# Column sums and gate broadcasts of a two-layer transformer block moved onto TensorE transposes and VectorE sums

## The chip, the cores and the metric

One core of one Trainium2 chip (trn2). The engines are TensorE (PE, with its weight loads listed apart as PEld), VectorE (DVE), ScalarE (ACT), GpSimd (POOL) and SyncE (SP), which issues the loads. The metric is the time of one execution on the device in microseconds (us), the median of several runs.

## The reference

Two residual blocks run one after the other over 256 tokens of width 1024, everything in fp32. Each block has several sub-blocks (FFN, short convolution, sparse attention, differential attention, grouped attention), and each of these is modulated by vectors that come from a conditioning vector `c` through a 1024 x 1024 slice of a large matrix:

```python
mod = (jax.nn.silu(c) @ ada_w[layer] + ada_b[layer]).reshape(B, 3, 3, D)
h = modulate_pre(x, g[0, 0], mod[:, 0, 0], mod[:, 0, 1])     # rms_norm(x)*(1+scale)+shift
y = swiglu_ffn(h, ffn_w_in[layer, 0], ffn_w_out[layer, 0])
x = x + weight * gate[:, None, :] * rms_norm(y, g_post)      # gated_post_add
...
mod = (cond_lat @ ada_w[i] + ada_b[i])[:, None, :]           # second block: shift, scale, gate x 2
modc = (cond_ctx @ ada_w[i] + ada_b[i])[None, None, :]       # the same matrix with a second vector
```

So there are 32 such products of a vector of 1024 with a 1024 x 1024 matrix, and eleven sub-blocks that use them as `shift`, `scale` and `gate`.

## The kernel before

Weights are streamed in units of 1 MB (128 x 2048 fp32) through a ring of three buffers `stage`. ScalarE rounds a unit to `w_hi` (fp32r, L821), VectorE forms the remainder `w_lo` (L1245), and TensorE makes each product out of three passes, `h_hi*w_hi`, `h_lo*w_hi` and `h_hi*w_lo`: L1948 to L1950 in the first half of a sub-block (`up`), L1999 in the second (`down`). The order on each engine is written out by hand, with semaphores between the engines (`lo_done`, `mid_done`, `ada_sum`, `ada_col` and others). The sub-blocks are, in order: s0 FFN, s1 convolution, s2 FFN, s3 key/value projection, s4 FFN, s5 sparse attention (nsa), s6 FFN, s7 differential attention (diff), s8 FFN over 512 rows, s9 grouped attention (gqa), s10 FFN. FFN `up` steps 0 to 8 are three steps of a loop body, executed once and then twice more in a loop.

**The modulation vectors.** For 23 of the vectors (those of s0, s1, s2, s4, s6 and s8) the product is accumulated by VectorE: eight operations `acc_ops` (L1290, L1292) over tiles 128 x 1024 of `ada`, each scaled by one element of the condition per partition, into a tile 128 x 1024 (`acc`, held in `gate_b`). The vector is the sum of this tile over its 128 partitions. `acc_sum` on TensorE makes this sum with eight matmuls, each with 128 columns of `acc` as its weights and four columns of ones as what moves through; it stands between two halves of a step of products. `acc_col` on VectorE then adds the bias to the eight columns and puts them into `modv` (L1306). In s8 there are two conditions, so each of its three vectors has two tiles and 16 matmuls. Four of the 23 vectors are `late`: their sum stands between two sub-blocks.

**The gates.** A sub-block's output is multiplied by a row of 1024 gate values that must stand on all partitions, while `modv` holds them as columns. VectorE multiplies the identity by each of the eight columns (`diag`, L1472, eight instructions), and TensorE multiplies a matrix of ones by `diag` in two matmuls of 512 columns (L1968), so that each row of the bank is the gate. ScalarE copies the two banks to `gate_b` (L979). This is done 12 times: once per sub-block but s3, and twice in s7 and s8. In an FFN the gate stands in the last `up` step, between products; in s5 and s9 it stands after the second `down` step.

## Time and profile before

| what | value |
|---|---|
| median of 3 runs | 2211.81 us (2211.53 to 2211.98) |
| profiled execution, from first to last instruction (the only time the profile gives for it) | 2215.9 us |
| busy: PE, DVE, ACT, POOL | 2109.6 us (95%), 1375.2 us (62%), 936.4 us (42%), 97.9 us (4%) |
| chain that ended last, by engine | PE 82%; DVE 8%; ACT 4%; DMA 3%; issue 2% |
| HBM read | 408.47 MB, 185 GB/s over the span |
| DMA share and rate from 0 to 50 us, from 50 to 300 us | 0.97 and 350 GB/s; 0.76 and 261 GB/s |

"Busy" is the time in which an engine executed anything. The chain that ended last goes from the last instruction back to what released each one; its shares say which engine's work set the end. A matmul in fp32 that is not a transpose stands as two records, one for each of its passes. Ends of matmuls are modelled, so the pace of TensorE is read from the distance between starts.

### The profile page before, as it was taken

The page shows a single profiled execution, that of the slowest core. Times are in us where ns is not written, and L with a number is a line of the kernel's source. Part 1 is how long each engine was busy: PE and PEld are TensorE (multiplying, and loading weights), DVE is VectorE, ACT ScalarE, POOL GpSimd, SP SyncE. Part 2 cuts the span into 40 slices and gives each one's busy share as a digit, 9 for nine tenths or more (in the row PEclk, how much of TensorE's full clock was granted, in tenths as well). Part 3 has the DMA queues.
Part 4 walks back from the last instruction along what each step waited for, and adds up shares of the span by engine and source line. Part 5 has one row for each costly group of instructions (what it writes and reads, how often), then busy time and mean ns, then how long its engine had stood idle before and what let it go on. Part 6 is the DMA issues. An engine that isn't in the chain of part 4 may idle for free.

```text
span 2215.9 us, 33686 instructions
## 1 busy us (share of the span) xinstructions
PE 2109.6 (95%) x13577; PEld 1849.4 (83%) x13577; DVE 1375.2 (62%) x2012; ACT 936.4 (42%) x1405; POOL 97.9 (4%) x142
## 2 busy tenths in 40 slices
PE   5999999999899999989999999989999999999999
PEld 3998898998899986459987997678888787977997
DVE  3767798677767674447755755866445334856454
ACT  4334435344533454444355445842122223554343
POOL 2000000000100001200001000010000000000000
PEclk8999999999999998889999999999999999999999
DMA  9887686886678756746854321024434232315553
GB/s 327 278 292 276 221 293 220 286 286 245 209 266 304 284 174 227 236 166 228 286 173 140 115 92 43 1 96 139 163 117 151 76 105 76 115 54 194 181 180 114
DMA packets 246618, 411.38 MB, mean 186 GB/s; under 512 B 10237, under 2 KB 191958, under 8 KB 246486
## 3 DMA queue, kind: packets, MB, share of 16 engines
q1 hardware_dynamic: 245888, 409.31, 54.3%
q8 instruction: 93, 1.52, 0.3%
q14 instruction: 40, 0.32, 0.0%
q10 hardware_dynamic: 597, 0.23, 0.0%
HBM read 408.47 MB, written 1.05 MB: 185 GB/s over the span
## 4 chain that ended last, share of the span: by engine, by line
PE 82%; DVE 8%; ACT 4%; DMA 3%; issue 2%; SPq 1%; POOL 1%; DVEq 0%; ACTq 0%
PE bank L1999 20%; PE bank L1948 14%; PE bank L1950 14%; PE bank L1949 14%; PE bank L2074 3%; PE bank L2076 3%; PE bank L2075 3%; PE bank L1900 2%; DVE w_lo L1245 1%; PE bank L1879 1%; DMA ada<-in_ada_w 1%; DVE gate_b L1292 1%; DMA xs<-in_ada_w 1%; PE bank L2178 1%; ACT w_hi L821 1%
## 5 line engine op out<-in xcount | busy, mean ns | idle before, releaser
L1245 DVE TENSOR_TENSOR w_lo<-stage,w_hi 128x2048 fp32r<-128x2048 f32 x255 | 584.6, 2294 | 444.6 <-ACT w_hi L821 443.8
L821 ACT CAST w_hi<-stage 128x2048 fp32r<-128x2048 f32 x255 | 485.5, 1905 | 654.0 <-PE bank L1950 240.7
L1948 PE MATMUL bank<-h_hi,w_hi 128*128 128x256 f32 (+1 forms) x2360 | 712.5, 302 | 2.6 <-ACT mid L994 2.6
L1950 PE MATMUL bank<-h_hi,w_lo 128*128 128x256 f32 (+1 forms) x2360 | 707.1, 300 | 0.0
L1949 PE MATMUL bank<-h_lo,w_hi 128*128 128x256 f32 (+1 forms) x2360 | 707.1, 300 | 0.0
L1948 PEld LDWEIGHTS bank<-h_hi,w_hi 128*128 128x128 f32 x2360 | 454.1, 192 | 19.1 <-issue 5.5
L1949 PEld LDWEIGHTS bank<-h_lo,w_hi 128*128 128x128 f32 x2360 | 454.0, 192 | 15.6 <-issue 1.9
L1950 PEld LDWEIGHTS bank<-h_hi,w_lo 128*128 128x128 f32 x2360 | 453.6, 192 | 14.0
L1999 PE MATMUL bank<-w_hi,h_hi 128*128 128x512 f32 x776 | 245.7, 394 | 8.3 <-DVE h_lo L1254 7.7
L1999 PE MATMUL bank<-w_hi,h_lo 128*128 128x512 f32 x776 | 244.0, 392 | 0.0
L1999 PE MATMUL bank<-w_lo,h_hi 128*128 128x512 f32 x776 | 244.0, 392 | 0.0
L1292 DVE SCALAR_TENSOR_TENSOR gate_b<-ada,cond,gate_b 128x1024 f32<-128x1024 f32 x182 | 231.7, 1283 | 5.5
L1999 PEld LDWEIGHTS bank<-w_hi,h_hi 128*128 128x128 f32 x776 | 145.3, 189 | 41.4 <-issue 11.3
L1999 PEld LDWEIGHTS bank<-w_lo,h_hi 128*128 128x128 f32 x776 | 146.8, 189 | 30.8
L1999 PEld LDWEIGHTS bank<-w_hi,h_lo 128*128 128x128 f32 x776 | 146.7, 189 | 30.9
L2074 PE MATMUL bank<-w_hi,h_hi 128*128 128x256 f32 (+1 forms) x552 | 159.4, 289 | 7.9 <-issue 4.3
L2075 PE MATMUL bank<-w_lo,h_hi 128*128 128x256 f32 (+1 forms) x552 | 157.7, 286 | 0.0
L2076 PE MATMUL bank<-w_hi,h_lo 128*128 128x256 f32 (+1 forms) x552 | 157.6, 285 | 0.0
L1752 DVE TENSOR_TENSOR mid<-silu_t,bank 128x256 f32 (+3 forms) x132 | 60.9, 463 | 150.5 <-PE bank L1950 150.5
L1191 ACT ACTIVATE silu_t<-bank 128x256 f32<-128x256 f32 (+1 forms) x132 | 54.5, 418 | 217.0 <-PE bank L1950 207.1
L2074 PEld LDWEIGHTS bank<-w_hi,h_hi 128*128 128x128 f32 x552 | 107.6, 195 | 9.3 <-issue 7.0
L2075 PEld LDWEIGHTS bank<-w_lo,h_hi 128*128 128x128 f32 x552 | 107.8, 195 | 0.0
(252 smaller groups left out, 2024.7 us busy)
## 6 DMA issues: line engine op xcount, KB each, us to landing
ada<-in_ada_w SPq DMA_DIRECT2D x114, 1024.0 KB, 5.4
stage<-in_ffn_w_in SPq DMA_DIRECT2D x88, 1024.0 KB, 8.7
stage<-in_ffn_w_out SPq DMA_DIRECT2D x44, 1024.0 KB, 5.1
stage<-in_ffn_w_gu SPq DMA_DIRECT2D x44, 1024.0 KB, 5.2
stage<-in_ffn_w_down SPq DMA_DIRECT2D x22, 1024.0 KB, 5.0
stage<-in_a_w_in SPq DMA_DIRECT2D x12, 1024.0 KB, 7.6
stage<-in_diff_w_in SPq DMA_DIRECT2D x12, 1024.0 KB, 5.5
ada<-in_kv_ada_w SPq DMA_DIRECT2D x8, 1024.0 KB, 5.6
```

The lines of the kernel that those rows point to most:

```text
L821: a.copy(w_hi[:, s, :], stage[:, s, :]).then_inc(hi_done, 1)
L1191: a.activation(silu_t[:, q, 0:T], bank[q][:, 0:T], ACT.Silu).then_inc(silu_done, 1)
L1245: v.tensor_tensor(w_lo[:, s, :], stage[:, s, :], w_hi[:, s, :].bitcast(F32), ALU.subtract).then_inc(lo_done, 1)
L1292: ins = v.scalar_tensor_tensor(out=acc[c], in0=w, scalar=cond[:, b, kk, c:c + 1], in1=acc[c], op0=ALU.mult, op1=ALU.add)
L1752: v.tensor_tensor(mid[:, bass.ds(o, T)], silu_t[:, q, 0:T], bank[2 + q][:, 0:T], ALU.mult).then_inc(mid_done, 1)
L1948: m.matmul(dst[:, 0:T], wh, h_hi[:, h0:h0 + T], start=(k == ks[0]), stop=False)
L1949: m.matmul(dst[:, 0:T], wh, h_lo[:, h0:h0 + T], start=False, stop=False)
L1950: ins = m.matmul(dst[:, 0:T], wl, h_hi[:, h0:h0 + T], start=False, stop=(k == ks[-1]))
L1999: ins = m.matmul(y_bank(T, tt, h)[:, :], a_[:, r:r + P], w_[:, slot, kc * D + h * 512:kc * D + (h + 1) * 512], start=first and n == 0, sto ...
L2074: m.matmul(dst, h_hi[:, r], w_hi[:, slot, c], start=(k == ks[0]), stop=False)
L2075: m.matmul(dst, h_hi[:, r], w_lo[:, slot, c], start=False, stop=False)
L2076: ins = m.matmul(dst, h_lo[:, r], w_hi[:, slot, c], start=False, stop=(k == ks[-1]))
```

## The change

1. `acc_sum` of the 19 vectors that are not late issues, for each tile, eight transposes of 128 x 128 (`acc` as weights, the identity moving) into two whole banks. `acc_col` gets a VectorE sum over the free dimension for each tile (`reduce_sum`, from 128 x 1024 in PSUM to 128 x 8 in `astat`), a wait of VectorE for that sum (`acc_red`), and then adds the bias as before. The banks used start at 4, formerly 5. The four late vectors stay as they were.
2. `gate` on TensorE issues eight transposes whose weights are one column of the gate vector read 128 times (step zero). VectorE's eight multiplications with the identity and the wait for them are gone; TensorE now waits for the gate vector itself (`G`, or `ada_col`).
3. One wait of TensorE for `cmp_kept` (a ScalarE copy out of bank 4) is added in the loop of s4.

```diff
+        def reduced(v):
+            late = [s["v"] + s["late"] for s in subs if s["late"]]
+            return len([x for x in made_by_dve(rv(v) + 1) if x not in late])
+        def is_late(v):
+            return v in [s["v"] + s["late"] for s in subs if s["late"]]
...
             def acc_col(vi, z, i=None):
                 dve.wait_ge(ada_sum, rv(vi) + (1 if i is None else i))
+                if not is_late(vi):
+                    for c in range(streams(vi)):
+                        src = bank_all[:, z + 2 * c:z + 2 * c + 2, :].rearrange("p b (k q) -> p (b k) q", q=P)
+                        ins = v.reduce_sum(flat_astat[:, 8 * c:8 * c + 8], src, AX_X)
+                    ins.then_inc(acc_red, 1)
+                    dve.wait_ge(acc_red, reduced(vi) + (0 if i is None else i - 1))
                 for c in range(streams(vi)):
-                    src = bank[z][:, 32 * c:32 * c + 32].rearrange("p (c j) -> p c j", j=4)[:, :, 0]
+                    src = flat_astat[:, 8 * c:8 * c + 8]
+                    if is_late(vi):
+                        src = bank[z][:, 32 * c:32 * c + 32].rearrange("p (c j) -> p c j", j=4)[:, :, 0]
...
-                    gv = modc[:, 2, 8 * st:8 * st + 8]
-                    dve.wait_ge(dve_s, t.at((tag, "G", st)))
-                for h in range(2):
-                    if st:
-                        dve.wait_ge(pe_s, t.at((tag, "gate", st - 1, h)))
-                    for k in range(4):
-                        ins = v.tensor_scalar(diag[:, h, k * P:(k + 1) * P], ident[:, :], gv[:, 4 * h + k:4 * h + k + 1], None, ALU.mult)
-                    t.done(ins, dve_s, (tag, "diag", st, h))
...
                     for c in range(KC):
-                        o = 32 * st + 4 * c
-                        ins = m.matmul(bank[z][:, o:o + 4], acc[st][:, c * P:(c + 1) * P], ones[:, 0:4], start=True, stop=True)
+                        if is_late(vi):
+                            o = 32 * st + 4 * c
+                            ins = m.matmul(bank[z][:, o:o + 4], acc[st][:, c * P:(c + 1) * P], ones[:, 0:4], start=True, stop=True)
+                        else:
+                            ins = m.transpose(bank[z + 2 * st + c // 4][:, c % 4 * P:(c % 4 + 1) * P], acc[st][:, c * P:(c + 1) * P], ident[:, :])
...
             def gate(s, tag, c):
+                if s["post"]:
+                    gv = modc[:, 2, 8 * c:8 * c + 8]
+                    pe.wait_ge(dve_s, t.at((tag, "G", c)))
+                else:
+                    gv = modv[:, mv(s, 2), 8 * c:8 * c + 8]
+                    pe.wait_ge(ada_col, max(rv(mv(s, 2)), rv(s["v"] + 2) if s["dv"] else 0) + 1)
                 for h in range(2):
                     if c:
                         pe.wait_ge(act_s, t.at((tag, "gateb", c - 1, h)))
-                    pe.wait_ge(dve_s, t.at((tag, "diag", c, h)))
-                    t.done(m.matmul(gate_bank(s, h, c)[:, :], ones[:, :], diag[:, h, :], start=True, stop=True), pe_s, (tag, "gate", c, h))
+                    for k in range(4):
+                        ins = m.transpose(gate_bank(s, h, c)[:, k * P:(k + 1) * P], gv[:, 4 * h + k:4 * h + k + 1].broadcast_to([P, P]), ident[:, :])
+                    t.done(ins, pe_s, (tag, "gate", c, h))
...
-                                    acc_col(s["v"], 5, i)
+                                    acc_col(s["v"], 4, i)
...
-                                also = {(0, 1): (lambda: acc_sum(s["v"], 5, i),)}
+                                also = {(0, 1): (lambda: pe.wait_ge(act_s, t.at("cmp_kept")) if after_kv(s) else None, lambda: acc_sum(s["v"], 4, i))}
```

**TensorE, third vector of s0** (step 9 of `up`). Before, the eight matmuls with four columns of ones; `gate_b` is the accumulated tile:

```order
L1949 MATMUL bank<-h_lo,w_hi 128x256
L1950 MATMUL bank<-h_hi,w_lo 128x256
L1900 MATMUL bank<-ones,gate_b 128x4 x8
L1948 MATMUL bank<-h_hi,w_hi 128x256
L1949 MATMUL bank<-h_lo,w_hi 128x256
L1950 MATMUL bank<-h_hi,w_lo 128x256
```

Now, eight transposes at the same place (the lines have moved by 13):

```order
L1962 MATMUL bank<-h_lo,w_hi 128x256
L1963 MATMUL bank<-h_hi,w_lo 128x256
L1913 MATMUL bank<-ident,gate_b 128x128 x8
L1961 MATMUL bank<-h_hi,w_hi 128x256
L1962 MATMUL bank<-h_lo,w_hi 128x256
L1963 MATMUL bank<-h_hi,w_lo 128x256
```

The number of instructions is the same; the columns that move are 128 in place of four.

**TensorE, gate of s0** (last `up` step). Before, two matmuls of 512 columns; `diag` is what VectorE wrote:

```order
L1949 MATMUL bank<-h_lo,w_hi 128x256
L1950 MATMUL bank<-h_hi,w_lo 128x256
L1968 MATMUL bank<-diag,ones 128x512 x2
L1948 MATMUL bank<-h_hi,w_hi 128x256
L1949 MATMUL bank<-h_lo,w_hi 128x256
```

Now, eight transposes of `modc`, which holds the gate vector:

```order
L1962 MATMUL bank<-h_lo,w_hi 128x256
L1963 MATMUL bank<-h_hi,w_lo 128x256
L1987 MATMUL bank<-ident,modc 128x128 x8
L1961 MATMUL bank<-h_hi,w_hi 128x256
L1962 MATMUL bank<-h_lo,w_hi 128x256
```

They are at the same place between the same products.

**VectorE, end of the convolution s1**. Before: the multiplications with the identity (L1472), the first half of a late vector (L1290, L1292), weight remainders, the column sum (L1306):

```order
L1464 SCALAR_TENSOR_TENSOR modc<-modv,cols 128x8
L1472 TENSOR_SCALAR diag<-ident,modc 128x128 x8
L1290 TENSOR_SCALAR gate_b<-ada,cond 128x1024
L1292 SCALAR_TENSOR_TENSOR gate_b<-ada,cond,gate_b 128x1024 x3
L1245 TENSOR_TENSOR w_lo<-stage,w_hi 128x2048
L1306 TENSOR_TENSOR modv<-bank,cols 128x8
L1245 TENSOR_TENSOR w_lo<-stage,w_hi 128x2048 x2
L1254 TENSOR_TENSOR h_lo<-mid,h_hi 128x512
```

Now:

```order
L1482 SCALAR_TENSOR_TENSOR modc<-modv,cols 128x8
L1300 TENSOR_SCALAR gate_b<-ada,cond 128x1024
L1302 SCALAR_TENSOR_TENSOR gate_b<-ada,cond,gate_b 128x1024 x3
L1255 TENSOR_TENSOR w_lo<-stage,w_hi 128x2048
L1311 TENSOR_REDUCE astat<-bank 128x8
L1324 TENSOR_TENSOR modv<-astat,cols 128x8
L1255 TENSOR_TENSOR w_lo<-stage,w_hi 128x2048 x2
L1264 TENSOR_TENSOR h_lo<-mid,h_hi 128x512
```

Eight instructions have gone ahead of the late vector, and one sum over 128 x 1024 (L1311) has come in behind the first of the three remainders.

## Rows read from the trace of the kernel before

**Rows 1.** Costliest groups by line: busy us, mean ns | idle before.

```profile
L1900 PE MATMUL bank<-ones,gate_b 128*128 128x4 f32 x416 | 48.8, 250 | 0.0
L1472 DVE TENSOR_SCALAR diag<-ident,modc 128x128 f32<-128x128 f32 x48 | 10.0, 282 | 0.2
```

**Rows 2.** PE in order of time, a column sum in s0: start us, us.

```profile
84.79 0.28 PE L1950 MATMUL bank<-h_hi,w_lo 128*128 128x256 f32 x1
84.91 1.84 PE L1900 MATMUL bank<-ones,gate_b 128*128 128x4 f32 x16
...
86.82 0.28 PE L1949 MATMUL bank<-h_lo,w_hi 128*128 128x256 f32 x1
```

**Rows 3.** PE in order of time, the gate of s0.

```profile
173.77 1.88 PE L1968 MATMUL bank<-diag,ones 128*128 128x512 f32 x4
...
175.61 0.28 PE L1949 MATMUL bank<-h_lo,w_hi 128*128 128x256 f32 x1
```

**Rows 4.** Line L1959, transposes of activations: ns min/median/max.

```profile
L1959 PE MATMUL bank<-ident,mid x208: 270/273/476, 14.6 to 2015.8; 128*128 128x128 f32 x104
```

**Rows 5.** PE in order of time, one run of such transposes.

```profile
19.37 1.09 PE L1959 MATMUL bank<-ident,mid 128*128 128x128 f32 x8
```

**Rows 6.** PE in order of time, two column sums in s8.

```profile
1570.13 3.63 PE L1900 MATMUL bank<-ones,gate_b 128*128 128x4 f32 x32
1573.62 0.49 PE L1948 MATMUL bank<-h_hi,w_hi 128*128 128x512 f32 x1
...
1640.65 4.62 PE L1900 MATMUL bank<-ones,gate_b 128*128 128x4 f32 x32
1645.13 0.77 PE L1948 MATMUL bank<-h_hi,w_hi 128*128 128x512 f32 x1
```

**Rows 7.** Windows of s8: busy us (count) by engine, PEclk, DMA share, GB/s.

```profile
1574.90:1578.20 3.30, 3.30 (x9) 2.59 (x8) 0.22 (x1) 0.00 (x0) 0.00 (x0) 0.50 0.00 0
1578.30:1581.60 3.30, 3.30 (x16) 2.73 (x15) 0.48 (x1) 0.00 (x0) 0.00 (x0) 1.00 0.00 0
...
1646.50:1649.80 3.30, 3.30 (x9) 2.56 (x8) 0.00 (x0) 0.00 (x0) 0.00 (x0) 0.50 0.00 0
```

**Rows 8.** Windows of s7, in which PE does nothing but transposes (L2312).

```profile
1431.50:1434.80 3.30, 3.30 (x18) 3.26 (x17) 3.30 (x6) 2.46 (x4) 0.00 (x0) 0.50 0.00 0
1434.90:1440.00 5.10, 4.08 (x25) 3.45 (x24) 1.96 (x3) 5.10 (x9) 0.00 (x0) 1.00 0.00 0
```

**Rows 9.** Line L1667, the sums (maxima) over banks: ns min/median/max.

```profile
L1667 DVE TENSOR_REDUCE astat<-bank x32: 681/952/1225, 1356.9 to 1419.9; 128x2 f32<-128x1024 f32 x16, 128x2 f32<-128x512 f32 x16
```

**Rows 10.** DVE in order of time in s0, a weight remainder.

```profile
109.85 2.29 DVE L1245 TENSOR_TENSOR w_lo<-stage,w_hi 128x2048 fp32r<-128x2048 f32 x1
```

**Rows 11.** PE in order of time, first product of that unit.

```profile
115.49 0.28 PE L1948 MATMUL bank<-h_hi,w_hi 128*128 128x256 f32 x1
```

**Rows 12.** DVE in order of time, end of s1.

```profile
318.55 2.29 DVE L1245 TENSOR_TENSOR w_lo<-stage,w_hi 128x2048 fp32r<-128x2048 f32 x1 [0.44 <-ACT w_hi L821]
...
326.39 0.42 DVE L1819 TENSOR_TENSOR mid<-silu_t,bank 128x256 f32<-128x256 f32 x1
```

**Rows 13.** PE in order of time, first `down` step of s1.

```profile
326.12 0.61 PE L1999 MATMUL bank<-w_hi,h_lo 128*128 128x512 f32 x2
326.87 0.50 PE L1999 MATMUL bank<-w_hi,h_hi 128*128 128x512 f32 x1
```

**Rows 14.** PE in order of time, the gate of s5.

```profile
975.83 1.88 PE L1968 MATMUL bank<-diag,ones 128*128 128x512 f32 x4
979.72 0.47 PE L1999 MATMUL bank<-w_hi,h_hi 128*128 128x512 f32 x1 [2.01 <-DVE h_lo L1254]
```

**Rows 15.** ACT in order of time, the second copy of that gate.

```profile
977.74 0.59 ACT L979 COPY gate_b<-bank 128x512 f32<-128x512 f32 x1 [0.27 <-PE bank L1968]
```

**Rows 16.** PE in order of time, the first instruction behind the first gate of s7.

```profile
1426.23 0.83 PE L2297 MATMUL bank<-mid 128*128 128x128 f32 x6
```

**Rows 17.** ACT in order of time beside it.

```profile
1424.66 0.63 ACT L1108 COPY mid<-bank 128x256 f32<-128x256 f32 x2
```

More of the change, by code:

```diff
@@ L112, in trace @@
         acc_s = sem("acc_s")
+        acc_red = sem("acc_red")
         part_done = [sem(f"part_done{i}") for i in range(3)]
@@ L1777, in _ @@
                         if s["dv"] and j == 9:
-                            acc_col(s["v"] + 2, 5)
+                            acc_col(s["v"] + 2, 4)
                         if s["nvec"] == 5:
@@ L1785, in _ @@
                         if j == 3:
-                            acc_col(s["v"], 5)
+                            acc_col(s["v"], 4)
                         split(u + 3 * j + 3)
@@ L2389, in _ @@
                     also = {}
-                    up_step(9, None, 2, (0, 2), False, {(0, 1): (lambda: acc_sum(s["v"] + 2, 5),)} if s["dv"] else None)
+                    up_step(9, None, 2, (0, 2), False, {(0, 1): (lambda: acc_sum(s["v"] + 2, 4),)} if s["dv"] else None)
                     if T == 256:
@@ L2405, in _ @@
                     up_step(1, None, 3, (0, 2, 6), False)
-                    up_step(2, None, 3, (0, 2, 6), False, {(1, 1): (lambda: acc_sum(v0, 5),)})
+                    up_step(2, None, 3, (0, 2, 6), False, {(1, 1): (lambda: acc_sum(v0, 4),)})
                     up_step(3, None, 3, (0, 2, 6), False, {(2, 0): (early_gate,)})
```

## The prediction

> **What bounds the kernel now.** I read the profile from the whole to the part. The busy shares and the chain that ended last come first: TensorE is busy 95% of the span and holds 82% of the chain, so a microsecond taken from TensorE is worth a microsecond wherever it has no wait close behind it. The groups by line show that the column sums are on that engine: 416 records [rows 1], that is 26 tiles x 8 matmuls x 2 passes. 22 of the 26 tiles change (16 with one stream in s0, s1, s2, s4 and s6, six in s8), and four late ones do not. TensorE in order of time then gives the price of one. Products start 0.12 us apart; the column sum starts at 84.91 and the second product behind it at 86.82 [rows 2]. Without the sum that product would start at 85.03, so the sum costs 1.79 us, although hardly any columns move: 16 passes, about 0.11 us apart. No wait stands around it. In the same way a gate costs 175.61 - 173.77 - 0.12 = 1.72 us [rows 3].
>
> **What a transpose costs.** The activations are transposed in fp32 by the same instruction: 26 tiles x 8 make exactly the 208 records of that line [rows 4], so a transpose has one pass, not two. Eight in a row stand for 1.09 us, the last of them 0.27 us long [rows 4, 5]: seven distances in 0.82 us, 0.117 each, and 8 x 0.117 = 0.94 us until the next instruction can start. That was at full clock with nothing to wait for; a run of 16 costs 1.88 us.
>
> **The terms on TensorE.**
> - 16 column sums of one stream: 1.79 - 0.94 = 0.85 each, 13.6 us.
> - Three vectors of s8, 32 passes each. At full clock one takes 1573.62 - 1570.13 = 3.49 us [rows 6] and would take 1.88: 1.61 each for two (the third vector stands like the first), 3.2 us. The one at 1640.65 takes 1645.13 - 1640.65 = 4.48 us [rows 6] since the clock falls within it: 2.6 us. Together 5.8.
> - The clock. Behind two of these three sums the granted clock is 0.50, that is 1.2 instead of 2.4 GHz: nine matmuls in 3.3 us where 16 run at full clock [rows 7]. That costs 3.3 x 7/16 = 1.4 us after 1574.9, and 4.7 x 7/16 = 2.1 us from 1645.1 to 1649.8. What TensorE did before was a sum of 3.5 us in which four columns moved per pass. In s7 TensorE does nothing but fp32 transposes from 1431.5 to 1434.8, at 0.50, and afterwards the clock is 1.00 [rows 8]. So transposes keep it up, and the 3.5 us come back.
> - Gates between products (s0, s2, s4, s6, s10 and both of s8, seven): 1.72 - 0.94 = 0.78 each, 5.5 us.
> - Gates of s5 and s9. Here TensorE stands still behind the gate: it starts at 975.83, and the next product at 979.72 waited for `h_lo` [rows 14]. The wait hangs on the gate itself. ScalarE copies both banks, the second at 977.74, only when the second matmul is done [rows 15], and then rounds what VectorE and TensorE wait for. With transposes the first bank is full after 3 x 0.117 + 0.27 = 0.62 us, the second after 7 x 0.117 + 0.27 = 1.09; the first copy, 0.59 us long, overlaps the second half, so the second copy starts about 1.1 us behind the gate's start instead of 1.91. That is 0.8 each, 1.6 us, and the stall of 2.01 us itself stays.
> - The first gate of s7. The matmuls behind it start at 1426.23 [rows 16], but their input has been copied at 1424.66 + 0.63 = 1425.3 [rows 17]: 0.9 us. Behind the second gate TensorE waits for VectorE until 1431.03, so this one gives nothing.
> - The gate of s1 gives nothing either. There TensorE stands before 326.87 until VectorE's `mid` of 326.39 is done [rows 12, 13], and VectorE works without a wait from 318.55, where it last waited for ScalarE's `w_hi` [rows 12]. That start moves by the 0.85 of the column sum ahead of it; the gate's 0.78 only makes the wait longer.
>
> Sum: 13.6 + 5.8 + 3.5 + 5.5 + 1.6 + 0.9 = 30.9 us.
>
> **The costs on VectorE.** Added are 22 sums over 128 x 1024 in PSUM. The trace has the same shape as a maximum over two banks, up to 1225 ns [rows 9]: 22 x 1.22 = 27 us. Removed are 96 multiplications: 48 of them take 10.0 us [rows 1], so eight take 1.67 and all of them 20 us. VectorE is busy 62%, so the sum of 7 us is covered as long as the single place is. The tightest place is the loop of the FFNs: column sum, four `acc_ops`, and behind them in VectorE's queue the weight remainders for which TensorE waits (`lo_done`). One of these ends at 109.85 + 2.29 = 112.14, and TensorE takes the unit at 115.49 [rows 10, 11]: 3.35 us in hand, which the new 1.22 us, plus the 0.85 by which TensorE comes earlier, do not use up. Were that cover gone, a column sum would cost what it adds there, 1.22 us. In s1 both meet: the eight multiplications (1.67) leave ahead of the late vector and the new sum (1.22) comes in, so that VectorE reaches its wait for `w_hi` no later. The queue of loads has the same slack: `acc_ops` free the `ada` ring, and SyncE issues weight loads behind those of `ada`; but at 261 GB/s, against 350 in the first 50 us, the DMA engines are not the bound, and a pace higher by 2% doesn't make them so. The wait for `cmp_kept` and the gate's wait for `G` or `ada_col` name work that ends microseconds earlier in TensorE's order; I price them at nothing.
>
> **What the trace does not show** is a weight load of one column read 128 times. Its lower bound is the dense transpose, 0.117 us; the nearest row above it is the pace of transposes at half clock, 3.3 / 18 = 0.18. I take the dense one, because as many elements go into the array and the other operand is the same identity; at 0.18 the cost is 96 x 0.07 = 6 us, which the upper end of the range holds.
>
> **The skill.** Rows 8 show the clock rising over transposes. The Trainium skill, "TensorE: Matmul & The Clock Gate", Part 4: PE-mode transpose, says the contrary: transposes do not count as busy time for the clock gate. It also gives about 275 ns for one, and the trace agrees (273), though their pace is what counts. By that rule the sum would lose the 3.5 us of clock, 27.4 in all; its hard form is the last rival.
>
> **The rivals.**
> - The clock behind the sums of s8 stays as it was: 30.9 - 3.5 = 27.4, that is 2184.4 us. Against it: rows 8. Chance 0.09.
> - VectorE's sum comes onto TensorE's path at each place, because a remainder or `mid` is late: 22 x 1.22 = 26.8 given back, 2207.7 us. For it: the sum stands ahead of everything else in VectorE's queue; against it: 3.35 us in hand. Chance 0.05.
> - The read with step zero is slow: at 0.34 us per gate transpose, three times the dense one, 96 x 0.22 = 21 us are given back, 2202 us. Nothing in the trace is near it. Chance 0.06.
> - Slower than before: the granted clock falls behind every run of transposes in the midst of products. The place is the 19 column sums and 12 gates, the price 1.4 us each as behind 1574.9, so 31 x 1.4 = 43 us against 30.9: 2224 us. It decides from 22 of the 31 places on. Against it: the clock rose over transposes [rows 8], and 1.8 us of passes with four columns, which stand there now, are followed by products that are still 0.28 us long, as at full clock [rows 2]. Chance 0.04. The rule of the Trainium skill's page named above would be its reason.
>
> **How the numbers follow.** The profiled execution has 2215.9 us, 4 us above the median of the runs; the sum is made on it and taken from the median: 2211.8 - 30.9 = 2180.9 us, chance 0.73 for this course, with 0.03 for mixtures. Its own spread comes from the clock, which falls at different instants at the ten boundaries between sub-blocks (1.4 to 2.1 us for one fall more or less) and from the pace of a transpose, which I read from one run (10% of it over 22 x 8 + 96 = 272 transposes is 3 us). With the first rival that makes 2172 to 2190. A measurement of this kernel can tell about 0.2%, 4.4 us: all but the last rival are faster by more.
>
> **What would show it.** Right: the new transposes in s0 start about 0.12 us apart, the product behind them comes 0.94 us after the first; no clock of 0.50 in s8 between 1540 and 1720; the new sum on VectorE at 1.2 us, and no new wait of TensorE for `w_lo` in the FFNs; in s1 a longer wait before the second half of the first `down` step; TensorE's busy time lower by about 28 us. Wrong: transposes with two records each, paces of 0.2 us for the gates, windows at 0.50 behind column sums or gates, or TensorE waiting for L1255 or for `modv`.

## The result, and the profile after

The changed kernel takes 2179.72 us (median of 4 runs, 2176.2 to 2183.14) beside 2211.67 for the kernel before on the same chip: ratio 0.9854, 95% interval [0.9836, 0.9872], so 32 us less (28 to 36). Measured a second time it was 2183.04 us, ratio 0.9869 [0.9849, 0.9889], 29 us less. The forecast was 30.9 less, 2180.9 us.

The profiled execution has a span of 2174.5 us, 41.4 less than the profiled one of before. That is 9 to 12 us more than the medians say, so some of it belongs to this pair of executions and not to the change. TensorE is busy for 2060.2 us (before 2109.6), VectorE for 1381.8 (1375.2).

The costliest groups by line, as in [rows 1]; line, operation, count | busy us, mean ns | idle before:

```profile
L1913 PE MATMUL bank<-ident,gate_b 128*128 128x128 f32 x176 | 22.3, 272 | 0.0
L1911 PE MATMUL bank<-ones,gate_b 128*128 128x4 f32 x64 | 7.4, 248 | 0.0
L1987 PE MATMUL bank<-ident,modv 128*128 128x128 f32 x48 | 6.2, 272 | 0.0
L1987 PE MATMUL bank<-ident,modc 128*128 128x128 f32 x48 | 6.2, 272 | 0.0
L1311 DVE TENSOR_REDUCE astat<-bank 128x8 f32<-128x1024 f32 x22 | 26.5, 1218 | 0.0
```

The 352 passes of 22 tiles are 176, one for each transpose, and the four late tiles are left with 64 (L1911). The 96 gate transposes (L1987) are in two halves, from `modc` and `modv`. VectorE's new sum takes 1218 ns.

TensorE in order of time in s0: the first column sum (answers to [rows 2]), the unit of [rows 11], and the gate (answers to [rows 3]).

```profile
82.47 1.04 PE L1913 MATMUL bank<-ident,gate_b 128*128 128x128 f32 x8
83.27 0.36 PE L1961 MATMUL bank<-h_hi,w_hi 128*128 128x256 f32 x1
83.47 0.28 PE L1962 MATMUL bank<-h_lo,w_hi 128*128 128x256 f32 x1
...
112.14 0.28 PE L1961 MATMUL bank<-h_hi,w_hi 128*128 128x256 f32 x1
...
168.57 1.03 PE L1987 MATMUL bank<-ident,modc 128*128 128x128 f32 x8
...
169.56 0.28 PE L1962 MATMUL bank<-h_lo,w_hi 128*128 128x256 f32 x1
```

Read it by differences. From the start of the sum to the second product behind it were 86.82 - 84.91 = 1.91 us [rows 2]; now 83.47 - 82.47 = 1.00. A column sum saves 0.91. Behind a gate the same distance was 175.61 - 173.77 = 1.84 [rows 3] and is 0.99: 0.85. And the lead of the changed kernel grows by just these steps. Its first sum starts 84.91 - 82.47 = 2.44 us earlier, before anything of the change has acted; the unit of [rows 11], one sum later, 115.49 - 112.14 = 3.35 earlier; the gate, three sums later, 173.77 - 168.57 = 5.20 earlier. Three sums are 2.76, 0.92 each. The other sums of one stream are no different: from the start of the sum to the first product behind it are 1.70 or 1.71 us at all 16 places of the kernel before, and 0.79 at all 16 now (here 82.47 to 83.27), 0.91 less.

TensorE in s8, its three column sums (the first two answer to [rows 6]), and the windows there (answers to [rows 7]; us, then busy (count) of PE, PEld, DVE, ACT, POOL, then the granted clock, DMA share, GB/s).

```profile
1544.02 1.91 PE L1913 MATMUL bank<-ident,gate_b 128*128 128x128 f32 x16
1545.69 0.48 PE L1961 MATMUL bank<-h_hi,w_hi 128*128 128x512 f32 x1
...
1611.07 1.91 PE L1913 MATMUL bank<-ident,gate_b 128*128 128x128 f32 x16
1612.73 0.47 PE L1961 MATMUL bank<-h_hi,w_hi 128*128 128x512 f32 x1
...
1678.15 1.91 PE L1913 MATMUL bank<-ident,gate_b 128*128 128x128 f32 x16
```

```profile
1546.00:1549.30 3.30, 3.30 (x16) 2.74 (x15) 2.29 (x1) 0.69 (x1) 0.00 (x0) 1.00 0.00 0
1613.00:1616.30 3.30, 3.30 (x16) 2.67 (x16) 2.29 (x1) 0.73 (x1) 0.00 (x0) 1.00 0.00 0
1490.00:1720.00 230.00, 227.51 (x1037) 188.93 (x1036) 125.37 (x104) 56.42 (x50) 0.00 (x0) 1.00 0.43 142
```

The first sum takes 1.67 us in place of 3.49, the second 1.66 in place of 4.48, and behind both the clock stays at 1.00 where it was 0.50: 16 matmuls in 3.3 us, not nine. The stretch from 1545.69 to 1611.07 is 65.38 us, against 1640.65 - 1573.62 = 67.03 before: one fall of the clock cost 1.65 us (I had worked out 1.4). The third sum of the kernel before is this one:

```profile
1712.75 3.63 PE L1900 MATMUL bank<-ones,gate_b 128*128 128x4 f32 x32
```

So the stretch behind the second sum was 1712.75 - 1645.13 = 67.62 us [rows 6] and is 1678.15 - 1612.73 = 65.42: the second fall cost 2.20 (worked out 2.1), and both 3.85.

TensorE at s1 (answers to [rows 13]), behind the gate of s5 (to [rows 14]) and behind the gates of s7 (to [rows 16]); in brackets the idle time and what ended it.

```profile
317.83 0.61 PE L2019 MATMUL bank<-w_hi,h_lo 128*128 128x512 f32 x2
319.87 0.73 PE L2019 MATMUL bank<-w_hi,h_hi 128*128 128x512 f32 x2 [1.42 <-DVE mid L1829]
...
952.62 1.04 PE L1987 MATMUL bank<-ident,modc 128*128 128x128 f32 x8
955.72 0.70 PE L2019 MATMUL bank<-w_hi,h_hi 128*128 128x512 f32 x2 [2.06 <-DVE h_lo L1264]
...
959.72 0.70 PE L2019 MATMUL bank<-w_hi,h_hi 128*128 128x512 f32 x2 [1.03 <-DVE h_lo L1264]
...
1400.19 1.06 PE L2317 MATMUL bank<-mid 128*128 128x128 f32 x8
1401.09 1.04 PE L1987 MATMUL bank<-ident,modv 128*128 128x128 f32 x8
1405.00 1.29 PE L2332 MATMUL bank<-ident,ada 128*128 128x128 f32 x5 [2.88 <-DVE ada L1705]
```

In s1 the lead was 326.12 - 317.83 = 8.29 us before the wait for `mid` and is 326.87 - 319.87 = 7.00 behind it. In s5 the gate's start to the stalled product is 3.10 us, before 3.89 [rows 14]; the stall is there as before. The second wait, of 1.03 us, is new: before, the clock was 0.50 from 981.0 to 984.2, behind the first wait, so the products there took longer and the next `h_lo` was done when it was needed. The lead is 979.72 - 955.72 = 24.00 us at the first wait and 983.96 - 959.72 = 24.24 at the second. In s7 the lead at the instruction behind the first gate is 1426.23 - 1400.19 = 26.04 us, and at the one that waits behind the second gate 1431.03 - 1405.00 = 26.03: the second gate gave nothing.

VectorE at the end of s1, and in step 9 of s0 (in order of time):

```profile
305.81 2.28 DVE L1255 TENSOR_TENSOR w_lo<-stage,w_hi 128x2048 fp32r<-128x2048 f32 x1
308.01 1.22 DVE L1311 TENSOR_REDUCE astat<-bank 128x8 f32<-128x1024 f32 x1
...
309.35 4.49 DVE L1255 TENSOR_TENSOR w_lo<-stage,w_hi 128x2048 fp32r<-128x2048 f32 x2
```

```profile
160.54 1.22 DVE L1311 TENSOR_REDUCE astat<-bank 128x8 f32<-128x1024 f32 x1
...
161.88 0.75 DVE L1300 TENSOR_SCALAR gate_b<-ada,cond 128x1024 f32<-128x1024 f32 x1
162.67 4.00 DVE L1302 SCALAR_TENSOR_TENSOR gate_b<-ada,cond,gate_b 128x1024 f32<-128x1024 f32 x3
166.58 0.16 DVE L1482 SCALAR_TENSOR_TENSOR modc<-modv,cols 128x8 f32<-128x8 f32 x1
```

The vector that the gate needs, `G` (L1482), is done at 166.74, and the gate starts at 168.57: 1.83 us in hand. The new sum stands 6 us ahead of it in the same queue.

**Where the 41 us of this pair come from.** The lead was there in part before the change acted (2.44 us at the first sum), and it grew again in the first part of s5, where nothing is changed. The windows show it, first of before, then of after:

```profile
10.00:60.00 50.00, 37.37 (x229) 26.16 (x225) 20.23 (x30) 20.60 (x34) 8.60 (x7) 0.80 0.87 312
845.00:975.00 130.00, 119.31 (x707) 65.57 (x707) 59.22 (x323) 52.82 (x176) 25.77 (x24) 0.80 0.63 215
```

```profile
10.00:58.00 48.00, 32.97 (x233) 23.52 (x234) 20.75 (x31) 20.45 (x33) 7.50 (x7) 0.89 0.91 325
828.00:952.00 124.00, 110.91 (x699) 60.45 (x699) 57.72 (x315) 51.66 (x176) 25.79 (x24) 0.86 0.65 223
```

The stretch of s5 is 130 us before and 124 after, at a mean granted clock of 0.80 and 0.86. By TensorE's own instructions the lead grows a little less: from 823.58 - 805.73 = 17.85 us ahead of this stretch to 975.83 - 952.62 = 23.21 at the gate of s5, 5.4 us. With 2.4 us at the start that makes 8 of the 41 us. Other places without a change add and take as well: 1.1 us around s3, 1.2 at the step from s4 to s5, 1.6 at the first `down` step of s8 (clock 0.50 from 1755.7 to 1759.1 before, 1.00 there now), then -2.1 ahead of the first gate of s7 and up to 0.5 either way at other boundaries. These come to about nothing together, so some 33 us are left for the change.

### The profile page after: what moved, and what is told of

It is laid out like the page before. It is cut to its first block, busy times and chain, and to the rows that moved or that the text cites. A ratio compares the mean times of both kernels' runs of the same rounds, so it can differ in the third digit from the quotient of the medians.

```text
span 2174.5 us, 33366 instructions
## 1 busy us (share of the span) xinstructions
PE 2060.2 (95%) x13449; PEld 1818.6 (84%) x13449; DVE 1381.8 (64%) x1938; ACT 935.4 (43%) x1405; POOL 96.8 (4%) x142
## 4 chain that ended last, share of the span: by engine, by line
PE 81%; DVE 9%; ACT 4%; DMA 3%; issue 2%; SPq 1%; POOL 1%; DVEq 0%; ACTq 0%
PE bank L2019 21%; PE bank L1961 14%; PE bank L1963 14%; PE bank L1962 14%; PE bank L2094 3%; PE bank L2095 3%; PE bank L2096 3%; DVE w_lo L1255 2%; DMA ada<-in_ada_w 2%; DVE gate_b L1302 1%; PE bank L1889 1%; DMA stage<-in_ffn_w_in 1%; PE bank L1913 1%; PE bank L2290 1%; ACT w_hi L831 1%
## 5 line engine op out<-in xcount | busy, mean ns | idle before, releaser
L1961 PE MATMUL bank<-h_hi,w_hi 128*128 128x256 f32 (+1 forms) x2360 | 708.0, 300 | 2.6 <-ACT mid L1004 2.6
L1961 PEld LDWEIGHTS bank<-h_hi,w_hi 128*128 128x128 f32 x2360 | 452.9, 192 | 16.9 <-issue 3.6
```

The lines of the kernel that those rows point to most:

```text
L1961: m.matmul(dst[:, 0:T], wh, h_hi[:, h0:h0 + T], start=(k == ks[0]), stop=False)
```

## The experiments

There are twelve runs, ten different kernels and two repeats, each in five rounds beside the kernel before, whose median was 2212.4 us, and 2212.9 in the last four. What the clock did is read from one profiled execution of each. All of them compute the whole output.

**The gates alone.** The kernel before with TensorE's `gate` from the change, and without VectorE's multiplications:

```diff
-                    for k in range(4):
-                        ins = v.tensor_scalar(diag[:, h, k * P:(k + 1) * P], ident[:, :], gv[:, 4 * h + k:4 * h + k + 1], None, ALU.mult)
-                    t.done(ins, dve_s, (tag, "diag", st, h))
...
-                    t.done(m.matmul(gate_bank(s, h, c)[:, :], ones[:, :], diag[:, h, :], start=True, stop=True), pe_s, (tag, "gate", c, h))
+                    for k in range(4):
+                        ins = m.transpose(gate_bank(s, h, c)[:, k * P:(k + 1) * P], gv[:, 4 * h + k:4 * h + k + 1].broadcast_to([P, P]), ident[:, :])
```

> The kernel before with the 12 gates alone changed (eight transposes of a column read with step zero; VectorE's eight multiplications gone). If the terms of the prediction hold, TensorE gains 0.78 us at seven gates, 0.8 at those of s5 and s9, 0.9 once in s7 and nothing in s1: 8.0 us, so about 2203.7 us, ratio 0.9964. If the read with step zero were slow (0.34 us a transpose) it would be slower than before by 13 us. If VectorE's missing multiplications were what matters, s1 would gain too: in this kernel VectorE has 1.67 us less and no new sum, so if VectorE sets the end of s1's gate step, the wait before the second half of its first down step still starts from ScalarE's w_hi and the gate of s1 gives 0.

Measured 2207.72 us, ratio 0.9977 [0.9961, 0.9993], so 5 us less (2 to 9); the 8 expected lie inside. In the trace its clock still falls behind the first and the third sum of s8:

```profile
1561.90:1565.30 3.40, 3.40 (x10) 2.63 (x9) 0.66 (x1) 0.00 (x0) 0.00 (x0) 0.50 0.00 0
1701.80:1705.20 3.40, 3.40 (x10) 2.63 (x9) 0.14 (x1) 0.00 (x0) 0.00 (x0) 0.50 0.64 177
```

**The sums alone.** The changed kernel with the two matmuls and the multiplications of the old gate (the same edit the other way round).

> The changed kernel with the gates as before (multiplications with the identity and two matmuls of ones). Terms of the prediction: 13.6 us for 16 column sums, 5.8 for s8's three and 3.5 for the clock behind them: 22.9 us, about 2188.8 us, ratio 0.9896. VectorE carries 27 us more and nothing less here; the rival that its sums come onto TensorE's path puts this near 2210 us. In s1 VectorE has 1.22 us more ahead of its wait for w_hi, which could show as a later first down step there, at most 0.8 us.

Measured 2190.32 us, ratio 0.9902 [0.9884, 0.992], 22 us less (18 to 26). The two halves add up: 5 + 22 = 27 beside 29 and 32 for both, with some 4 us of uncertainty on each.

**The sums of s8 alone**, with the old gates:

```diff
+        def is_late(v):
+            return v in [v_ for s in subs if s["dv"] and s["n"] != 8 for v_ in range(s["v"], s["v"] + s["nvec"])]
```

> As sum_only, but with transposes and VectorE sums in s8 alone; the sums of s0, s1, s2, s4 and s6 are matmuls with ones. The size term alone is 5.8 us, with the clock term of 3.5 it is 9.3: about 2202.4 us, ratio 0.9958. If the clock falls behind runs of 16 transposes as well, it is 5.8 us or less, about 2205.9 us, and windows with a granted clock of 0.50 stand between 1550 and 1720 us. The rest (16 sums) is then 13.6 us by difference with sum_only.

Measured 2203.33 us, ratio 0.9958 [0.994, 0.9975], 9.3 us less (5.5 to 13). The three sums of s8 and all of its `up` steps are at full clock:

```profile
1490.70:1739.70 249.00, 246.51 (x1104) 203.15 (x1104) 134.80 (x123) 59.86 (x54) 0.00 (x0) 1.00 0.42 139
```

This window ends just ahead of the first `down` step. There the clock is 0.50 from 1739.9 to 1743.1, behind a wait of 2.49 us for `h_lo`, as it was in the kernel before from 1755.8 to 1759.0 behind the same wait. That fall has nothing to do with the sums: the changed kernel has the wait (2.48 us) without the fall, and gates alone or sums alone have a fall there.

**What the falls of the clock go with.** Is it that the run of passes got shorter, or that columns move in them? The kernel before, in which only the ones-matmuls of s8 move 128 columns instead of four; they keep their two passes each, and so their number (as in the changed kernel they start at bank 4, and the loop of s4 has the wait for `cmp_kept`):

```diff
-                        ins = m.matmul(bank[z][:, o:o + 4], acc[st][:, c * P:(c + 1) * P], ones[:, 0:4], start=True, stop=True)
+                            ins = m.matmul(bank[z + 2 * st + c // 4][:, c % 4 * P:(c % 4 + 1) * P], acc[st][:, c * P:(c + 1) * P], ones[:, :], start=True, stop=True)
```

> The kernel before with one change in s8 alone: its column sums are still matmuls with ones, two passes each, but 128 columns of ones move instead of four. A pass stands for about 0.11 us either way, so the sums are as long as before (3.5 us) and only what moves per pass is different. Theory: the nearly empty passes let the granted clock fall behind them; with full passes no window at 0.50 stands between 1500 and 1720 us, and the time is 3.5 us lower, about 2208.5 us. Rival: the clock falls for the length of the interruption of the products, whatever moves; then windows at 0.50 stay there and the time is that of before.

Measured 2206.84 us, ratio 0.9975 [0.9963, 0.9987], 5.5 us less (3 to 8), and no clock below 1.00 in this window, which reaches over all three sums:

```profile
1497.10:1750.00 252.90, 251.67 (x1152) 208.48 (x1150) 126.70 (x117) 58.31 (x52) 0.00 (x0) 1.00 0.42 137
```

```profile
1571.12 3.73 PE L1917 MATMUL bank<-ones,gate_b 128*128 128x128 f32 x32
1574.61 0.48 PE L1965 MATMUL bank<-h_hi,w_hi 128*128 128x512 f32 x1
```

So in s8 it is neither the length of the sum nor the number of its passes, but what moves in them. A sum takes 1574.61 - 1571.12 = 3.49 us, to the hundredth what it took with four columns [rows 6], and the 3.5 us that were forecast for the clock come back without a transpose in the sums. One trace alone could be luck, since the falls do not stand behind the same two sums in the two kernels that have them. But they stand behind four of the six sums with four columns (the kernel before and the gates alone), and behind none of the 36 sums of s8 in the other twelve profiled executions, in all of which 128 columns move.

**How much room the VectorE sum has.** Each sum two times and four times, into columns of `astat` that nobody reads:

```diff
+                        for r in range(3):
+                            o = 16 + 8 * (3 * c + r)
+                            v.reduce_sum(flat_astat[:, o:o + 8], src, AX_X)
                         ins = v.reduce_sum(flat_astat[:, 8 * c:8 * c + 8], src, AX_X)
```

> The changed kernel with each of the 22 VectorE sums done twice (the extra one into columns that nothing reads). In the changed kernel's trace the tightest weight remainder of s0 ends 2.11 us before TensorE takes its unit (3.36 before the change), so another 1.22 us is still covered in the FFNs; only in s1, where VectorE sets the end of the gate step, about 1.1 us should show. Theory: within 2 us of the changed kernel, 2179.7 to 2182. The rival that VectorE's sums lie on TensorE's path says 22 x 1.22 = 27 us more, about 2207 us.

> As sums_x2 with each sum done four times: 3.66 us more at each place against 2.11 to 2.2 us in hand. Theory of the cover: TensorE now waits about 1.5 us for a remainder twice in each of s0, s2, s4 and s6 (12 us), and 2.7 us in s1; s8 with its steps of 22 us stays covered: about 14 us more than the changed kernel, 2190 to 2197 us, and TensorE's waits for the line of w_lo rise from 5 us to some 15. If the cover is larger than I read it, no change; if the sums were on the path from the first, 80 us more.

Twice: 2188.29 us, ratio 0.9879 [0.986, 0.9898]. The median is 6 us above the 2182 that I had expected at most; by the ratios it is 2 to 6 us more than the changed kernel in its two measurements, which is hardly more than they can tell. The waits of TensorE show 1.5 us of it:

```profile
PE bank L1990 <- DVE modc L1485: 1.5, 3, 0.7
```

Four times: 2218.94 us, ratio 1.0022 [1.0011, 1.0034], slower than the kernel before, and 34 to 37 us above the changed one (by the same ratios) where 14 were expected. The waits (us in total, times, longest):

```profile
PE bank L1964 <- DVE w_lo L1255: 14.6, 10, 3.2
...
PE bank L1990 <- DVE modc L1485: 7.6, 3, 3.1
```

The first is the wait that I had looked for, in ten places with 14.6 us where I had worked out 12 in eight. The second I had not: the gate waits for `G`. And behind it the clock falls:

```profile
178.72 1.70 PE L1990 MATMUL bank<-ident,modc 128*128 128x128 f32 x8 [3.11 <-DVE modc L1485]
```

```profile
179.00:183.00 4.00, 4.00 (x24) 4.00 (x22) 4.00 (x3) 3.10 (x5) 0.00 (x0) 0.57 1.02 393
```

In 4 us of products of 0.12 us each stand 24. Eight transposes take 1.70 us there, against 1.03. So I took the two places apart: four sums only in the loop passes, and only for the third vector of each FFN (step 9).

```diff
-                        for r in range(3):
+                        for r in range(0 if i is None else 3):
```

```diff
-                        for r in range(3):
+                        for r in range(3 if i is None and vi in [q["v"] + 2 for q in subs if q["dv"]] else 0):
```

> Each VectorE sum four times, but only in the eight loop passes of the FFNs (8 of the 22 sums, 8 x 3.66 us more VectorE work), the others once. If the weight remainders are what is late, the four FFNs with loops lose about 4.5 us each, as read between 100 and 145 us from the kernel with all sums fourfold: 18 us, 2198 us, with waits of TensorE for w_lo as there, and no wait of the gates for G, since the third sum is single again. If every repeated sum costs alike, it is 39 x 8/22 = 14 us, 2194 us, and these waits would be fewer.

> Each VectorE sum four times only for the third vector (step 9 of s0, s2, s4 and s6, and the one of s8), the others once. In the changed kernel G is ready at 166.74 us and the gate of s0 starts at about 169.9: 3.2 us in hand against 3.66 us more work. If nothing but this one slack counts, the gates wait 0.5 us each and the kernel loses 2 to 4 us: 2182 to 2184 us. If the gate waits for G by itself as long as in the kernel with all sums fourfold (3.1 us and a clock that falls behind it, 1.4 us more), it loses 4 x 4.5 = 18 us: 2198 us.

> The changed kernel once more, as the base for the kernels beside it. Expected 2176 to 2183 us, ratio to the kernel before 0.985 to 0.987.

The changed kernel once more, their base, is the 2183.04 us given above. The loop alone: 2203.8 us, ratio 0.9966 [0.995, 0.9982], 21 us more than that base, with 18 expected. The third vector alone: 2188.61 us, ratio 0.988 [0.986, 0.99], 2 us more by the ratio and 6 by the medians, where 2 to 4 were expected. Their waits, first of the loop alone, then of the third vector alone:

```profile
PE bank L1964 <- DVE w_lo L1255: 13.6, 8, 3.1
```

```profile
PE bank L1990 <- DVE modc L1485: 4.4, 3, 1.5
```

Each place has its own cover, and each kernel shows only its own wait. The time of the first would not show this by itself. Its loop passes are 12 of the 22 sums and not 8, as the expectation has it, for s8 has a loop too, with two sums in each pass:

```profile
L1313 DVE TENSOR_REDUCE astat<-bank 128x8 f32<-128x1024 f32 x36 | 41.7, 1215 | 0.0
```

So its rival, that every repeated sum costs alike, says 39 x 12/22 = 21 us, just what was measured. The trace decides against it: all eight waits are in s0, s2, s4 and s6, and in s8 the first and the third sum are 1705.75 - 1571.00 = 134.75 us apart, against 1678.15 - 1544.02 = 134.13 in the changed kernel, though 12 of the 36 extra sums of VectorE lie between them. (The expectation put the start of the gate at 169.9; it is 168.57, so there are 1.83 us in hand and not 3.2; 3.66 - 1.83 = 1.83 was to be expected and 1.5 is what stands there.) Together the two cost 24 to 26 us, and all sums fourfold 34 to 37. In that kernel the gates of s0 and s4 wait 3.11 and 3.00 us instead of 1.45 each, and behind both waits the clock is 0.50 for 3.4 us. That is 3.2 us of waits and, at the 1.65 to 2.20 us that a fall cost above, some 4 us of clock, an estimate of 7 of the 10. That the loop has made VectorE late already is the likely reason, but it is not shown: in s2 the gate waits 1.45 us there, as it does alone. The rest of the difference I leave open: that kernel also repeats the sums of s1 and s8, and executions scatter by 5 us.

**The stall that stayed.** In s5 and s9 the gate stands after the second `down` step, and TensorE then waits 2.06 and 1.03 us for `h_lo`. The changed kernel with the gate in the middle of that step:

```diff
                 step(0, None)
-                step(1, None)
                 if s["kind"] in ("nsa", "gqa"):
+                    ready(1)
+                    products(1, None, 0)
                     gate(s, tag, 0)
+                    products(1, None, 1).then_inc(w_used, 1)
+                else:
+                    step(1, None)
```

> The changed kernel with the gates of s5 and s9 in the middle of the second down step instead of behind it. In the changed kernel TensorE waits 2.06 and 1.03 us behind the gate of s5, 2.13 and 0.93 behind that of s9, since ScalarE's copies, which wait for the gate, stand ahead of the rounding that the third step needs. Theory: the gate's place makes these stalls, and 2.7 us earlier it removes most of them: 4 to 6 us less than the changed kernel, about 2175 us. Rival: the stalls come from the rounding and the remainder themselves (0.62 + 0.69 us and the weight split before them) and stay: no change from 2179.7 us. A second rival: TensorE waits in front of the gate for G, which VectorE computes behind the weight remainder, and gives the gain back.

> The version with the gates of s5 and s9 in the middle of the second down step once more, beside the changed kernel on the same chip. If the stall behind those two gates (2.06 + 1.03 and 2.13 + 0.93 us) is what it takes away, it is 4 to 6 us faster than the changed kernel in the same call. If its lead of 8 us over the first measurement of the changed kernel was the place where the clock fell in the executions, the two are within 2 us.

Measured 2171.84 us, ratio 0.9836 [0.9812, 0.986], and 2170.72 us, ratio 0.9823 [0.9801, 0.9846], each time faster than the changed kernel in its own measurement (0.9854, 0.9869). The first pair of intervals overlaps; the second, taken side by side, does not. The trace shows one wait of 0.61 us where there were two (and so in s9):

```profile
950.16 1.03 PE L1987 MATMUL bank<-ident,modc 128*128 128x128 f32 x8
...
957.27 0.70 PE L2019 MATMUL bank<-w_hi,h_hi 128*128 128x512 f32 x2 [0.61 <-DVE h_lo L1264]
```

That is 2.5 us for each of the two gates, 5 of the 4 to 10 us measured. It and the next one are the fastest versions that I found.

**The late four as well**, on top of that version: their sums by transposes too (the bank that they use between two sub-blocks moves from 5 to 4).

> The changed kernel with the gates of s5 and s9 in the middle of the second down step, and the four late vectors by transposes and VectorE sums as well. Gate place alone: 2171.8 us. The late sums stand between two sub-blocks where TensorE waits for VectorE anyway (2.3 to 2.6 us right behind), so theory says their 4 x 0.85 us give nothing, and VectorE's 1.22 us come behind the first remainders of the next sub-block: 2171 to 2173 us. Rival: full passes at the boundaries keep the clock up there, 1.4 us or more at each: 2165 to 2169 us.

Measured 2174.22 us, ratio 0.9831 [0.9811, 0.9851]: no gain that can be told from nothing, and none of the 1.4 us or more at each boundary that the rival in the expectation gave to the clock.

## Why the prediction was right

It had the mechanism, the places and the sum; point by point, by its own steps:

- **"16 column sums of one stream", 0.85 each.** Measured 0.92. The pace of the transpose was read from a run of 1.09 us [rows 5]; in the midst of products eight take 1.04, (1.04 - 0.27) / 7 = 0.11 us apart. At that size 15 of the 16 are 13.8 us. For the one in s1 see below.
- **"Three vectors of s8", 5.8 us.** 3.49 - 1.67 = 1.82 and 4.48 - 1.66 = 2.82; with the third like the first 6.5.
- **"The clock", 3.5 us.** Right. The two falls gave back 1.65 and 2.20 us, no 0.50 is left between 1490 and 1720 us, and three kernels bear it out: the two with changed passes in s8 lose the falls, the one with changed gates keeps them. With this the first rival falls, and the Trainium skill's rule in "TensorE: Matmul & The Clock Gate", Part 4: PE-mode transpose, has no support here: the clock did not sink over the 16 transposes in s8 (1.00 before and behind them), nor was it lower behind those of s0, where a product takes 0.28 us as before. (The 275 ns of the same section, with which the prediction found the trace to agree, are told of bf16; the 273 here are of fp32.)
- **"Seven gates between products", 0.78 each.** Measured 0.85 in s0, 6 us for all. The step-zero read costs nothing: the weight loads of the gates have a median of 137 ns, those of the dense transposes 140 (rows below). The third rival falls with its whole price.
- **"Gates of s5 and s9", 0.8 each, the stall stays.** Exactly so, 3.89 - 3.10 = 0.79 and a stall of 2.06. The moved gate shows what the stall hung on.
- **"The first gate of s7", 0.9, the second nothing.** The second is right to 0.01 us. The first gate's run of eight starts at 1399.32 and the next instruction at 1400.19, which is 0.87 us; before it was 1424.51 to 1426.23, 1.72 us. That saves 0.85.
- **"The gate of s1 gives nothing".** Right, the wait swallowed it: the lead shrinks by 1.29 us over a wait of 1.42. But the step beneath it, that VectorE's start there "moves by the 0.85 of the column sum", is wrong. VectorE waited for ScalarE's `w_hi` [rows 12]; now it doesn't wait at all from 305.81 to its `mid`, since the new sum of 1.22 us stands in this chain. It is VectorE that sets the time. The last of the three remainders starts at 309.35 + 4.49 - 2.29 = 311.55, 7.00 us earlier than before [rows 12], which is the lead of TensorE behind the wait. So the wait hides the sum's gain too, in part: TensorE has a lead of 6.52 us at the start of s1's products (247.94 against 254.46), and of 7.00 behind this wait, so that 0.5 of the 0.92 are left.
- **VectorE's sums are covered.** Right for the change as it is: no wait of L1961 for `w_lo`, none of the gate for `modc`. The second rival falls. But the argument looked at one place. It named `w_lo` (3.35 us in hand) and priced the gate's wait for `G` at nothing because it "ends microseconds earlier"; those are 1.83 us. Twice the sum already makes the gates wait (0.7 us at most), four times the sum turns the gain of the whole change into a loss.
- **The rival on the other side**, the clock falling behind each run of transposes: did not happen at any of the 31 places of the changed kernel. The one fall close behind a gate, in s7, starts at 1405.0 with the end of a wait of 2.88 us, and stood there before the change too [rows 8].

With the sizes measured the sum is 13.8 + 0.5 + 6.5 + 3.9 + 6.0 + 1.6 + 0.9 = 33.2 us, which fits the 33 that are left of the pair of profiles, and the 29 and 32 of the medians. That 2180.9 lies between 2179.7 and 2183.0 is finer than either the terms or the runs can bear: the column sums, s8, the clock and the gates each came out 0.4 to 0.7 us larger than forecast.

The weight loads of the two kinds of transposes in the changed kernel (ns min/median/max, first and last start):

```profile
L1913 PEld LDWEIGHTS bank<-ident,gate_b x176: 138/140/144, 82.4 to 1679.7; 128*128 128x128 f32 x176
```

```profile
L1987 PEld LDWEIGHTS bank<-ident,modc x48: 134/137/137, 168.5 to 1105.8; 128*128 128x128 f32 x48
```

TensorE's busy time fell by 49 us where 28 were forecast. A TensorE at half clock is busy too, for twice as long, so that this number has the luck of the clock in it and was a poor one to foretell.

## What to carry to other kernels

Price an instruction on the bounding engine by the distance between the starts around it, and not by the columns that it moves: here 16 passes of four columns cost 1.79 us, eight passes of 128 columns 0.88. Work that goes to the other engine is free only as far as the nearest thing behind it in that queue for which the bounding engine waits; list them all with what each has in hand (here 3.35 us for the weights and 1.83 for the gate's vector), for the smallest of them decides. And before a difference of two profiles is given to a change, check how much of it stands at places that the change doesn't touch: here 8 of 41 us.

## What the runs showed of the hardware

- The granted clock was 0.50 at four of the six column sums of s8 with 32 passes of four columns (two profiled executions): for 3.4 us behind three of them, for 6.8 us from within the fourth. It fell behind none of three when the same 32 passes moved 128 columns, and behind none of 33 with 16 transposes. The 16 sums of 16 passes with four columns that the kernel before has between products had no fall behind them.
- The first `down` step of s8 comes behind a wait of 2.48 or 2.49 us in the kernel before, in the changed one and in the one with sums in s8 alone. In the first and the last the clock was 0.50 behind it, in the changed one 1.00: the same wait, with and without a fall.
- Widening those passes from 4 to 128 columns cost no time (3.49 us for 32 of them either way).
- A weight load that reads one column 128 times takes 137 ns at its median, a dense one 140.
- Executions of the same kernel scatter by 5 us and more (2175.1 to 2185.7 for the changed kernel in its second measurement) although the work is fixed. In the traces the clock differs between executions at the start and in the first part of s5: the second profile of the changed kernel has 0.80 from 10 to 60 us, like the kernel before, and 0.89 in the stretch of s5.

```profile
10.00:60.00 50.00, 37.25 (x229) 26.20 (x230) 20.29 (x30) 20.63 (x34) 8.61 (x7) 0.80 0.87 312
829.00:953.00 124.00, 110.76 (x721) 61.05 (x720) 57.69 (x315) 53.42 (x177) 25.79 (x24) 0.89 0.67 232
```
